# One stage for projection and sparse attention, keys scored four sequences at once, and an output projection begun inside a recurrence

## What is computed

```python
z = h @ ab_w_in                      # q, k, v, 16 index queries qi, index key ki, weights wi, and zb
ki = rmsnorm(ki)
score = sum_h relu(qi_h . ki) * wi_h # index score of each key; the best 64 (prompt) or 256 (sample) stay
ya = softmax over the kept keys of (q . k) / 8, times v     # 8 heads; samples read a paged cache of 1024 keys
yb = rwkv7(zb)                       # recurrence over 8 heads, chunks of 64 tokens, head norm, gate
y = concat(ya, yb) @ ab_w_out        # 1024 x 1024
x = x + rmsnorm(y)
```

## Time and profile before

| | us |
|---|---|
| median of 3 runs | 1500.51 |
| lowest, highest | 1495.41, 1504.65 |
| the profiled execution | 1502.46 |
| its span | 1500.7 |
| PE busy in it | 1427.5 |
| DVE busy in it | 1091.8 |
| ACT busy, POOL busy in it | 328.2, 333.1 |
| mean granted clock of PE | 0.968 of full |

### The profile page before, as it was taken

How to read it: one execution, slowest core, us unless ns; L and a number is a source line. 1 busy time by engine, 2 the same in 40 slices (tenths; PEclk the granted TensorE clock), 3 DMA queues, 4 the chain that set the end, 5 groups by cost and what they waited for, 6 DMA issues and landing times.

```text
span 1500.7 us, 28281 instructions
## 1 busy us (share of the span) xinstructions
PE 1427.5 (95%) x11458; PEld 1296.5 (86%) x11458; DVE 1091.8 (73%) x1407; ACT 328.2 (22%) x651; POOL 333.1 (22%) x280
## 2 busy tenths in 40 slices
PE   6999999997998996899999999999999999999997
PEld 6999999994343595899999999999997668999997
DVE  7977677654977735788778688768579577887764
ACT  3111102003333443231111221111202362211110
POOL 2533112001100012244321053321200002443310
PEclk9999999998898998899999999999999879999998
DMA  8443543655785102454417344426163314444142
GB/s 311 147 164 110 201 144 122 215 178 209 254 283 213 38 4 99 176 198 161 162 73 260 132 169 168 168 82 243 40 216 113 121 57 189 158 160 163 70 157 90
DMA packets 62795, 233.24 MB, mean 155 GB/s; under 512 B 9051, under 2 KB 18592, under 8 KB 45676
## 3 DMA queue, kind: packets, MB, share of 16 engines
q1 hardware_dynamic: 50426, 224.56, 42.0%
q10 hardware_dynamic: 11554, 6.37, 1.4%
q0 software_dynamic: 720, 0.97, 0.2%
HBM read 225.54 MB, written 6.10 MB: 154 GB/s over the span
## 4 chain that ended last, share of the span: by engine, by line
PE 50%; DVE 5%; POOL 2%; ACT 1%; issue 1%; DMA 1%; POOLq 0%; DVEq 0%; SPq 0%
PE psum L191 15%; PE psum L193 15%; PE psum L192 15%; DVE x L393 1%; DMA ring<-in_w_gu 1%; DVE ring_r L186 1%; DVE hidden_hi L389 1%; DVE pair_hi L177 1%; DVE rstd L297 1%; POOL hidden L305 0%; POOL hidden L307 0%; PE psum L351 0%; DMA ring<-in_w_cd 0%; PE psum L235 0%; PE psum L236 0%
## 5 line engine op out<-in xcount | busy, mean ns | idle before, releaser
L191 PE MATMUL psum<-x_hi_r,pair_hi 128*128 128x288 f32 x1736 | 515.5, 297 | 16.5 <-DVE ring_r L186 13.2
L193 PE MATMUL psum<-x_hi_r,ring_r 128*128 128x288 f32 x1736 | 514.6, 296 | 0.0
L192 PE MATMUL psum<-x_lo_r,pair_hi 128*128 128x288 f32 x1608 | 474.8, 295 | 0.0
L191 PEld LDWEIGHTS psum<-x_hi_r,pair_hi 128*128 128x128 f32 x1736 | 328.3, 189 | 18.6 <-DVE ring_r L186 13.7
L186 DVE TENSOR_TENSOR ring_r<-ring,pair_hi 128x2048 fp32r<-128x2048 f32 (+1 forms) x127 | 339.1, 2670 | 4.3
L193 PEld LDWEIGHTS psum<-x_hi_r,ring_r 128*128 128x128 f32 x1736 | 327.8, 189 | 0.0
L192 PEld LDWEIGHTS psum<-x_lo_r,pair_hi 128*128 128x128 f32 x1608 | 303.4, 189 | 0.3
L191 PE MATMUL psum<-hidden_hi_r,down_hi 128*128 128x288 f32 x704 | 208.4, 296 | 0.0
L192 PE MATMUL psum<-hidden_r,down_hi 128*128 128x288 f32 x704 | 207.7, 295 | 0.0
L193 PE MATMUL psum<-hidden_hi_r,down_r 128*128 128x288 f32 x704 | 207.0, 294 | 0.0
L177 DVE CAST pair_hi<-ring 128x2048 fp32r<-128x2048 f32 (+1 forms) x126 | 160.5, 1274 | 12.4 <-DMA ring<-in_w_gu 11.1
(11 more groups left out here) (544 smaller groups left out, 1835.6 us busy)
## 6 DMA issues: line engine op xcount, KB each, us to landing
ring<-in_w_gu SPq DMA_DIRECT2D x88, 1024.0 KB, 4.8
down<-in_w_down SPq DMA_DIRECT2D x64, 704.0 KB, 4.3
ring<-in_w_ab SPq DMA_DIRECT2D x18, 1024.0 KB, 5.1
ring<-in_w_cd SPq DMA_DIRECT2D x12, 1024.0 KB, 6.2
ring<-in_cache_k SPq DMA_DIRECT2D x32, 256.0 KB, 5.2
index_keys<-in_cache_k SPq DMA_DIRECT2D x32, 256.0 KB, 4.1
index_keys<-in_cache_i ACTq DMA_DIRECT2D x64, 64.0 KB, 2.7
eight_pages_ds<-in_cache_v SPq DMA_DIRECT2D x16, 256.0 KB, 6.3
```

Source lines behind the costliest of these rows:

```text
L191: pe.matmul(out, w_hi, x_hi, start=start, stop=False)
L192: pe.matmul(out, w_hi, x_lo, start=False, stop=False)
L193: return pe.matmul(out, w_lo, x_hi, start=False, stop=stop)
```

## The change

Four edits. The projection becomes the head of `dsa_stage`, in one block with the stages before it; the values' first tile is made around the sums for ki's norm, the second one 3 matmuls at a time between the steps of index scores, the third one after them. `key_scores` takes four sequences at heads 2 and 6, in place of two at heads 1, 3, 5 and 7, and SP's loads of keys and values are regrouped for that. The quarters of the merge are moved by DVE copies and not by DMAs. And the output projection gets a `JoinedOut`: in the recurrence's end its four pairs are sent and split and four of its eight tiles are made (PSUM banks 7, 0, 1, 6), and `out_stage` makes the other four behind the barrier. To make room, several buffers of the recurrence change places, the initial states (s0t) load later, and POOL's first loads wait for the last index step. In the second mixer only semaphores are renamed.

```diff
-def ab_in_stage(c, z, vtok, idx, pre):
...
+            project_pe(c, pe, z_done, npairs, first, pre)
+            token_rstd_pe(c, pe, v_sum)
+            values_in(0, range(2))
             pe.wait_ge(S["ki_sq"], 1)
             pe.matmul(B[0][:, 0:NT], c.half_ones[:, :], kisq[:, :], start=True, stop=True).then_inc(S["ki_sum"], 1)
...
+            values_in(0, range(2, KT))
             pe.wait_ge(S["ki_done"], 1)
+            pe.wait_ge(S["wi_done"], 1)
+            index_scores(0)
+            for n in range(KT):
+                values_in(1, range(n, n + 1))
+                if n < 7:
+                    index_scores(n + 1)
+            values_in(2, range(KT))
...
+            pe.wait_ge(v_done, 3)
             for n in range(12):
...
-            def key_scores(b0):
+            def key_scores(g):
...
-                for b in (b0, b0 + 1):
+                four = range(4 * g, 4 * g + 4)
+                for b in four:
                     pe.wait_ge(kv_landed[KEY_SLOTS[b]], 128 * KEY_LOADS[b])
...
-                if h % 2:
-                    key_scores(h - 1)
+                if h in (2, 6):
+                    key_scores(h // 4)
```

The queue of loads (sync), the merge of the sorted quarters (vector):

```diff
+            sp.wait_ge(c.pair_done, first + npairs)
+            load("cache_k", 0, KEY_SLOTS[0])
             load("cache_v", 1, VALUE_SLOTS[1])
             idx.read_numbers(sp, c, 4, 5)
+            sp.wait_ge(c.pair_done, first + npairs + 2)
+            load("cache_k", 1, KEY_SLOTS[1])
...
-            load_halves("cache_k", 4, KEY_SLOTS, 2)
             idx.read_numbers(sp, c, 7)
-            load_halves("cache_k", 6, KEY_SLOTS, 4)
-            load_halves("cache_v", 2, VALUE_SLOTS, 6)
-            load_halves("cache_v", 4, VALUE_SLOTS, 8)
+            for u in range(2):
+                sp.wait_ge(S["kv_used"], 2 + 2 * u)
+                for b in range(4, 8):
+                    load("cache_k", b, KEY_SLOTS[b], range(4 * u, 4 * u + 4))
+            for u in range(2):
+                sp.wait_ge(S["kv_used"], 6 + 2 * u)
+                for b in range(2, 6):
+                    load("cache_v", b, VALUE_SLOTS[b], range(4 * u, 4 * u + 4))
...
-                dve.wait_ge(S["q_moved"], 160)
+                dve.tensor_copy(moved[quarter(0)], sq[quarter(1), 8:QW])
+                ln(dve.tensor_copy(moved[quarter(2)], sq[quarter(3), 8:QW]))
```

The end of the recurrence (sync, vector, scalar, tensor):

```diff
-        c.store(sp, c.outs["shift"], zlast[:, :, :])
+        sp.dma_start(c.outs["shift"], zlast[:, :, :]).then_inc(out.slot_free, 16)
+        sp.wait_ge(S["dve_grp"], 15)
+        send_pairs(c, sp, c.ins["w_ab_out"], 0, 1)
...
         sp.wait_ge(S["y_sum"], 5)
-        send_pairs(c, sp, c.ins["w_ab_out"], 0, 2)
+        sp.wait_ge(S["ub_done"], HP)
+        send_pairs(c, sp, c.ins["w_ab_out"], 1, 3)
...
+            if it == 2:
...
+                mask(dve, c.whi[:, out.first % RING], c.ring[:, out.first % RING]).then_inc(c.pair_masked, 1)
+            if it == 3:
...
+                low_bits(dve, c.ring_lo[:, out.first % RING], c.ring[:, out.first % RING], c.whi[:, out.first % RING]).then_inc(c.pair_split, 1)
...
         sample_state(1)
-        dve.wait_ge(S["var_sd"], 1)
-        dve.reciprocal(rows8, rows8).then_inc(S["var_rows"], 1)
+        for k_ in range(4):
+            low_part(k_)
+        dve.wait_ge(S["root_done"], 2)
+        dve.reciprocal(rows8, rows8).then_inc(S["inverse_done"], 1)
         sample_state(2)
-        sample_state(3)
+        split_pair(c, dve, out.first, 1)
         for h in range(HP):
             dve.wait_ge(S["var_all"], h + 1)
...
+            dve.tensor_tensor(ymix[:, 4 + h], f3[:, h], f1[:, h], ALU.add).then_inc(out.ymix_made, 1)
+            if h:
+                low_part(3 + h)
+        low_part(7)
+        sample_state(3)
+        dve.wait_ge(out.slot_free, 16)
+        split_pair(c, dve, out.first, 2)
+        split_pair(c, dve, out.first, 3)
...
+        for k_ in range(4):
+            act_mask(act, c.xhi[:, k_], ymix[:, k_]).then_inc(out.ymix_high, 1)
         for h in range(HP):
             act.wait_ge(S["yc_done"], h + 1)
...
+        act.wait_ge(S["var_all"], HP)
+        for h in range(HP):
+            act.wait_ge(out.ymix_made, 2 + h)
+            act_mask(act, c.xhi[:, 4 + h], ymix[:, 4 + h]).then_inc(out.ymix_high, 1)
...
+        for n in (0, 1):
+            for k_ in range(4):
+                out.product(pe, n, k_)
+        pe.wait_ge(S["inverse_done"], 2)
         for h in range(HP):
-            pe.matmul(B[h][:, 0:NT], pair_rows[:, h], rows8, start=True, stop=True).then_inc(S["var_all"], 1)
+            spread(h)
+        for n in (2, 3):
+            for k_ in range(4):
+                out.product(pe, n, k_)
+        for k_ in range(4, KT):
+            for n in range(4):
+                out.product(pe, n, k_)
```

More of the change, by code:

```diff
@@ L723, in project_dve, with project_values @@
             split_pair(c, dve, first, u + AHEAD)
-def project_values(c, pe, pair, tile_done, tiles=(0, 1, 2)):
+def project_values(c, pe, pair, tile_done, tiles=(0, 1, 2), ks=range(KT)):
     pe.wait_ge(c.pair_split, pair + 2)
@@ L730, in project_values @@
         t0, n = TOK[i]
-        for k in range(KT):
+        for k in ks:
             cols = slice(t0, t0 + n)
@@ L1596, in _, with tensor, values_in, index_scores @@
             rk.sample_decays(pool)
-        @block.tensor
-        def _(pe):
+        def tensor(pe):
+            def values_in(i, ks):
+                project_values(c, pe, first + npairs, lambda i, mm: mm.then_inc(*((v_sum, 1) if i < 2 else (c.pair_done, 2))), (i,), ks)
+            def index_scores(i):
+                if i >= 2:
+                    pe.wait_ge(S["ip_rel"], 2 * i - 2)
+                for e in range(2):
+                    for t in range(2):
+                        p_ = (i + t) % 2
+                        mm = pe.matmul(B[(2 * i + t) % 4][:, e * TP:(e + 1) * TP], qz_src[half(p_), 2 * (i // 2) + e, t * P:(t + 1) * P],
+                                       ki[half(p_), 0:TP], start=True, stop=True)
+                        if e == 1:
+                            mm.then_inc(S["ip_sum"], 1)
+            project_pe(c, pe, z_done, npairs, first, pre)
+            token_rstd_pe(c, pe, v_sum)
+            values_in(0, range(2))
             pe.wait_ge(S["ki_sq"], 1)
@@ L1858, in _, with vector @@
             rk.chunks_out(act)
-        @block.vector
-        def _(dve):
+        def vector(dve):
             def ln(ins):
                 c.link(dve, "dve", ins)
+            project_dve(c, dve, z, z_done, npairs, npairs + 2, first, pre)
             dve.wait_ge(S["par_loaded"], 112)
@@ L2803, in vector @@
                 low_bits(dve, ymix_lo[:, k], ymix[:, k], c.xhi[:, k]).then_inc(ymix_split, 1)
-        for u in range(own // 2, RING):
+        for u in range(joined.pairs_split if joined is not None else 0, RING):
             if joined is not None and u == RING - 1:
```

201 lines of the change are left out of this document (122 added, 79 removed).

## The result

The changed kernel takes **1492.45 us** (median of 6 runs, 1490.46 to 1495.68) against 1501.19 us before (6 runs, 1495.41 to 1504.65). The ratio is 0.9945, with a 95% interval of 0.9923 to 0.9968: 8.7 us or 0.6% less. Forecast were 1485 and a range of 1476 to 1495. The time lies in the range, 7.5 us above the forecast, and somewhat over half of the forecast gain of 15.8 us came.

The account below looks back on a forecast made before the run. PE was taken to bound the kernel outside the first mixer; inside it the limit moves from engine to engine. Terms 11.2 - 3.5 + 8.1 = 15.8 us, from a median of 1500.51 to 1485 us; range 1476 to 1495.

Parts of the forecast that it names:

- Projection and index scores: Stretch before the heads: with both in one stage, PE runs without a hole and the heads begin 11.2 us earlier.
- changes of shape: Interleaved value and index matmuls: each switch between matmul shapes costs PE 0.2 us; 16 switches, 3.2 us.
- Keys in fours: Attention heads: scoring four sequences per pass saves PE 14 us, costed at nothing because DVE is the bound there.
- Cost 3.5 us: Attention heads: loss from PE at half clock behind idle holes, 2.5 us before head 7 and 1.0 at mask spreads.
- two partial bursts: On the way to head 7: PE's half-clock spells after idling, taken as 2.5 us; a 4 us burst loses 1.9.
- My own sign of failure: Attention: the prediction is wrong if `select` comes later behind the heads' start than 57 us.
- The end of the recurrence: From the recurrence's means to the output stage's tail: early output tiles and splits win 8.1 us, 44 us instead of 52.
- 25.4 us together: End of the recurrence: DVE's previous 11.9 us, eight low parts and three splits, from 582.25 to 607.6 us.
- rival (c): End of the recurrence: DVE and PE wait for each other at three meetings, about 6 us lost; 1491, chance 0.09.
- Rival (b): Attention: keys late for the first four sequences, each us beyond 391 delaying head 3; five late gives 1490, chance 0.09.
- (d): Attention: loads of four sequences become the bound and the kernel gets slower; 1522 at 155 GB/s, chance 0.06.
- (a): Attention: PE's clock stays up or its holes lie beside DVE's work; 1479, chance 0.20.

Follow-up runs that it names:

- experiment 1: Changed kernel with the end of the recurrence as it was before (no output tiles, low parts or splits inside it); 1498.04 us, ratio 0.9984 to the kernel before.
- experiment 6: Changed kernel with most of POOL's work beside DVE at the mixer's end left out (results not valid); ratio 0.9935 to the kernel before.
- experiment 7: Changed kernel with the next stage's first two weight pairs loaded ahead of the barrier and the last products reordered; ratio 0.9925 to the kernel before.
- experiment 5: Changed kernel with 8 extra groups of unused products in each of TensorE's two holes in attention; 1488.92 us, ratio 0.9920 to the kernel before.
- experiment 2: Changed kernel with key scores in pairs again at heads 1, 3, 5, 7 and the old load order; ratio 0.9932 to the kernel before.
- experiment 10: Changed kernel with key scores in pairs and the samples' state products on ACT instead of POOL; 1487.78 us, ratio 0.9895 to the kernel before.
- experiment 8: Changed kernel with 8 extra product groups per TensorE hole, state products on ACT and early loads of the next weights; 1481.13 us, ratio 0.9875 to before.
- experiment 9: Changed kernel with 8 extra product groups per TensorE hole and state products on ACT, without early loads; 1486.46 us, ratio 0.9899 to the kernel before.
- experiment 4: Changed kernel with 16 extra groups of unused products in each of TensorE's two holes in attention; ratio 0.9988 to the kernel before.

## Why the prediction was right and where it was wrong

Three terms missed in one direction, by 3.3, 1.1 and 3.8 us, and one by 0.6 us in the other. That the time still lies in the range is owed to the width of the range, in which the clock alone had 0 to 7 us.

**Projection and index scores: right.** DVE's wait before the norm of ki is 2.66 us (said: about 3), the heads start at 378.82 (said: 379.4), 11.8 us earlier (said: 11.2), and PE ends that stretch: DVE waited 3.99 us for it. The changes of shape cost no more than the 0.2 us each that I read from the rows: a step of index scores with three value products takes 1.95 us, where 1.06 for the step and 3 x 0.235 for the products make 1.76. The reading of the Trainium skill by which they would cost double (TensorEngine Tiling (Array Packing), Key Properties) did not show: the heads would have come at 382 us.

**Keys in fours: the mechanism right, the term mis-sized.** That 14 us of saved work are worth nothing, that head 7 is waited for longer (5.00 us; said: about 4), and that no load is late, all came. The step that failed is "Cost 3.5 us", 2.5 on the way to head 7 and 1.0 at the spreads. Measured: 3.5 on the way to head 7 (55.3 us behind the heads' start, before 51.8) and 3.3 at `select` and the spreads, together 6.8 in this profile and 7.8 to 8.2 in experiments 1, 6 and 7, which have the same attention. Experiment 5 shows that it is the clock. My bounds of 0 to 7 us held the value of this profile, and not those of experiments 1, 6 and 7. My choice in them was wrong because I counted two partial bursts, where the clock is 0.50 from 407 to 422 us and again from 438 to 466. The kernel before has it for 4 us near 398 and from 458 on. Why it fell later there is open: with the last pair of key scores in its old place (experiments 2 and 10) it falls at 444 us. My own sign of failure, `select` later than 57 us behind the heads' start, came (436.61 us, 57.8). A further 1.1 us went between the shift and the means, for which my sum had no term. The clock is 0.87 in the last 38 us there, 0.96 before: it is 0.54 from 557 to 568 us, where the kernel before has 1.00 up to 564. The profiles agree. Experiments 5, 8, 9 and 10, with one such fall of about 4 us like the kernel before, take 116.3 to 116.5 us; 1, 2 and 6, with about 10 us at 0.50 like the changed kernel, take 117.2 to 117.4; 4 and 7, with two shorter falls, take 117.2 and 118.1. Why the clock stays down longer in some, with the same work, no run singles out; that stays open. The Trainium skill (TensorE: Matmul & The Clock Gate, What's actually happening) puts the ramp's penalty under 1% of a typical span. What this change added to it, 6.8 to 8.2 us, is 0.5%, within that; what the ramp costs in the whole kernel no run here shows. The rule bounds the loss, and does not find it.

**The end of the recurrence: one term of the sum mis-sized.** The barrier is 1.7 us (606.79 to 608.44) as I took it, TensorE's tiles end at 606.2 (said: 606 to 608), and the tail stands on splits. But means to tail is 47.6 us and not 43.8: 4.3 to 4.7 us won and not 8.1. The step that failed is "25.4 us together": it took 28.5, since I priced DVE's splits and low parts by rows in which POOL rests, and put them beside POOL's products. With POOL spared it takes 25.8, and means to tail is 2.7 us less of the 3.8 missing (experiment 6), in part behind the barrier. For the rest, a wait of 1.50 us for ACT's first masks is my rival (c) in small, one meeting of its three. And the tail's last step was named wrongly for this kernel: not the third pair's load, but the first one's (landed at 613.75) and three splits in a row set it. The third pair's is only 1 us behind it, as experiment 7 shows.

**The sum.** 11.84 - 6.76 - 1.13 + 4.33 = 8.28 us at the tail. Rival (b), late keys, did not come, nor did (d): the key products waited 0.2 us for a load, once, and rates of 379 to 396 GB/s were reached where I had reckoned with 336. (a), the clock that stays up, is what experiment 5 made: worth 6.9 us in the stretch, and still 1488.92 us and not 1479, since the end of the recurrence kept its cost.

## What to carry to other kernels

Work taken off an engine that waits anyway can cost time, where what comes next on that engine then runs at half clock, as here: look at what comes next, and price it at half clock. When an instruction is moved beside another engine's, price it from a row with the same neighbour, DVE beside POOL above all. And a load that had 8 us to spare can be the bound after a reorder of 7 us, since its start moves later and its use moves earlier.

## What the runs showed of the hardware

**DVE and POOL stop each other.** The subtraction from 588.77 us starts 0.88 us before POOL's product ends (587.68 + 1.97) and takes 0.74 us longer than 2.29; the one from 600.30 overlaps 0.89 us and takes 0.74 longer; the mask from 617.72 overlaps 0.74 and takes 0.61 longer. So DVE loses nearly the whole overlap. The one that is already at work is not slowed: the mask from 613.75 us takes 1.23 us, its usual time, though POOL's sum starts inside it at 614.01; it is that sum which takes 1.63 us and not 0.81. In experiment 7 POOL's sums take 1.81 us each beside DVE. That agrees with the Trainium skill (SBUF — State Buffer, SBUF: two separate sides), where the port that the two share is held for a whole instruction and the other is blocked.

**The granted clock is not the same from run to run.** Kernels with one and the same attention had a wait of 0, 1.60, 1.38 or 2.04 us at head 3 (the changed kernel, experiments 1, 6 and 7). Of two kernels that are the same up to there, the changed one has clock 1.00 from 386.8 to 390.8 us and experiment 4 has 0.50, both behind 4 us in which TensorE was busy 2.18 us. And with 8 extra groups the clock stayed at 1.00 up to the spreads in one profile and not in two others.
